# Two gated input stages of a float32 transformer kernel: their last four tiles by halves of the tokens

## The reference

```
for i in range(2):
    hn = rms_norm(h, norm_mixer[i])
    h = h + mixer_i(hn)                                  # gla, then fox
    h = h + (p[i] @ ple_proj[i]) * sigmoid(rms_norm(h, ple_norm[i]) @ ple_gate[i])
return rms_norm(h, final_norm)
```

## Time and profile before

| | |
|---|---|
| median of 3 runs | 2327.85 us (2324.41 to 2327.87) |
| profiled execution: time, span | 2328.21 us, 2326.0 us |
| mean granted TensorE clock | 0.975 of full speed |
| TensorE busy | 2200.5 us (95%) |
| VectorE busy | 1205.2 us (52%) |
| ScalarE busy | 856.5 us (37%) |
| GpSimd busy | 554.3 us (24%) |
| chain that ended last | TensorE 83%, VectorE 11%, issue 4%, ScalarE 2% |

### The profile page before, as it was taken

One profiled execution on the slowest core, in us unless ns is written; L12 is line 12 of the kernel. 1 busy time (PEld: TensorE's weight loads), 2 busy tenths in 40 slices (PEclk: granted clock), 3 DMA queues, 4 the chain that ended last, 5 costly groups with the idle time before them and its releaser, 6 DMA issues.

```text
span 2326.0 us, 29165 instructions
## 1 busy us (share of the span) xinstructions
PE 2200.5 (95%) x11168; PEld 1853.8 (80%) x11168; DVE 1205.2 (52%) x1488; ACT 856.5 (37%) x1295; POOL 554.3 (24%) x292
## 2 busy tenths in 40 slices
PE   4999999999999699999899979999999999999996
PEld 4778888988887598898778868888888888877885
DVE  6963332543331724334345454566666667676744
ACT  3136653112021323323322123446546546544311
POOL 1322221333333122222233222211111111111520
PEclk9999999999999699999999989999999999999998
DMA  8112222112331211101131121111111011012201
GB/s 338 53 46 73 73 72 73 55 37 89 137 136 46 82 36 46 37 28 46 36 138 44 46 99 56 37 46 36 45 54 43 29 54 45 27 45 101 81 19 73
DMA packets 36660, 154.59 MB, mean 66 GB/s; under 512 B 4161, under 2 KB 4161, under 8 KB 35810
## 3 DMA queue, kind: packets, MB, share of 16 engines
q1 hardware_dynamic: 23840, 93.52, 11.6%
q10 hardware_dynamic: 12738, 59.87, 7.2%
HBM read 128.15 MB, written 21.04 MB: 64 GB/s over the span
## 4 chain that ended last, share of the span: by engine, by line
PE 83%; DVE 11%; issue 4%; ACT 2%; DMA 0%; DVEq 0%; SPq 0%; ACTq 0%
PE psG L311 21%; PE psG L312 21%; PE psG L313 21%; PE psA L311 3%; PE psA L313 2%; PE psA L312 2%; PE psA L1884 1%; PE psA L1883 1%; PE psA L1858 1%; PE psA L1784 1%; DVE M L871 1%; PE psA L399 1%; DVE AL L824 1%; DVE AL L849 1%; PE psA L1867 1%
## 5 line engine op out<-in xcount | busy, mean ns | idle before, releaser
L311 PE MATMUL psG<-AH,WH 128*128 128x512 f32 x2108 | 856.8, 406 | 40.3 <-DVE AL L849 15.3
L312 PE MATMUL psG<-AL,WH 128*128 128x512 f32 x2108 | 831.8, 395 | 0.0
L313 PE MATMUL psG<-AH,WL 128*128 128x512 f32 x2108 | 830.8, 394 | 0.0
L298 POOL TENSOR_SCALAR WH<-RAW 128x1024 fp32r<-128x1024 f32 x144 | 165.3, 1148 | 1685.3 <-PE psG L311 1195.7
L311 PEld LDWEIGHTS psG<-AH,WH 128*128 128x128 f32 x2108 | 401.7, 191 | 124.7 <-issue 28.0
L313 PEld LDWEIGHTS psG<-AH,WL 128*128 128x128 f32 x2108 | 401.3, 190 | 88.1
L312 PEld LDWEIGHTS psG<-AL,WH 128*128 128x128 f32 x2108 | 402.9, 191 | 69.5
L300 POOL TENSOR_TENSOR WL<-RAW,WH 128x1024 fp32r<-128x1024 f32 x144 | 389.2, 2703 | 12.0
L2183 DVE TENSOR_TENSOR FTL<-PF,FTH 128x512 fp32r<-128x512 f32 x192 | 112.8, 588 | 129.2 <-ACT FTH L2058 127.2
L2051 ACT ACTIVATE PF<-psA,PB 128x512 f32<-128x512 f32 x192 | 111.3, 580 | 91.6 <-PE psA L1886 52.1
L2193 DVE RECIPROCAL FDR<-psA 64x128 f32<-64x128 f32 x128 | 118.2, 939 | 32.1 <-PE psA L313 30.5
(11 more groups left out here) (331 smaller groups left out, 2961.3 us busy)
## 6 DMA issues: line engine op xcount, KB each, us to landing
RAW<-w_tiles SPq DMA_DIRECT2D x144, 512.0 KB, 3.5
gates<-SIG ACTq DMA_DIRECT2D x16, 512.0 KB, 2.9
park<-X ACTq DMA_DIRECT2D x2, 4096.0 KB, 11.1
CB<-fox_c ACTq DMA_DIRECT2D x16, 512.0 KB, 4.3
X<-xT SPq DMA_DIRECT2D x4, 1024.0 KB, 11.9
WADA_SCALE<-w_ada SPq DMA_DIRECT2D x1, 4096.0 KB, 24.0
WADA_SHIFT<-w_ada SPq DMA_DIRECT2D x1, 4096.0 KB, 34.0
WADA_GATE<-w_ada ACTq DMA_DIRECT2D x1, 4096.0 KB, 16.4
```

Source lines behind the costliest of these rows:

```text
L298: nc.gpsimd.tensor_scalar(WH[:, i, :], RAW[:, i % RAW_SLOTS, :], 1.0, 0.0, ALU.mult, ALU.add).then_inc(w_high, 1)
L311: first = nc.tensor.matmul(out, wh, xh, start=start, stop=False)
L312: nc.tensor.matmul(out, wh, xl, start=False, stop=False)
L313: return first, nc.tensor.matmul(out, wl, xh, start=False, stop=stop)
```

## The change

In each of the two gated stages the first four tiles stay as they were. The last four are taken by halves of the tokens: tokens 0 to 511 of tiles 4 to 7, then tokens 512 to 1023 of tiles 4 to 7 (`step`). Each half tile is 24 + 6 matmuls, and a unit's two banks serve as two buffers of one half tile each. All four weight slots hold these tiles until their second halves; `tile_begun` is counted at the first tile's early half and at the late halves of the others.

The early half's norm is made while TensorE goes through the late half: its sums (4 blocks) stand after chunk 5 of the late half of tile 4, its spread (4 transposes) after chunk 1 of the late half of tile 5. DVE and ACT then make, between the late half's gates, the early half of the next operand (layer 0: `TN`, `AH`, `AL`) or of the final rows (layer 1), called `first(n)`.

After layer 0 the forget tile and the first q tile are also taken by halves, q two chunks behind. The late half's sums stand after chunk 3 of the early half, its spread after chunk 6; the late halves of the chunks are filled after that. After layer 1 sums, root and spread of the late half follow the last matmul, then the 8 late half rows; SP stores 16 half chunks, the early ones first. Some semaphores are merged or dropped (one name for the waits that only order POOL's and DVE's queues, `x_early` for `x_loaded`).

```diff
+    LO, HI = slice(0, HALF), slice(HALF, S)
+    WHOLE = KC // 2
+    def pe_half_sums(src, h, at):
+        for n in range(NB // 2):
+            s = (NB // 2 * h + n) * P
+            l = nc.tensor.matmul(psA[:, 2, at + n:at + n + 1], src[:, s:s + P], mat("ones")[:, 0:1], start=True, stop=True)
+        return l
+    def pe_half_spread(h):
+        for n in range(NB // 2):
+            m = NB // 2 * h + n
+            l = nc.tensor.transpose(psA[:, h, n * P:(n + 1) * P], RC[:, m:m + 1].to_broadcast([P, P]), mat("ident"))
+        return l
...
+    def pe_ple_halves(pe, layer, t0, u0):
+        gate, prod = 2 * (u0 % 2), 2 * ((u0 + 1) % 2)
+        def free(i, x):
+            if i < 2:
+                pe.wait_ge(psum_free, u0 + 2 * WHOLE - 1 + x)
+            elif i < 6:
+                pe.wait_ge(ph_free, 8 * layer + 2 * (i - 2) + 1 + x)
+            else:
+                pe.wait_ge(psum_free, u0 + 2 * (i - 2) + 1 + x)
+        for i in range(KC):
+            j, cols, b = step(i)
+            full = ph_full if i < 4 else psum_full
+            if i < 4:
+                pe.wait_ge(w_split, t0 + j + 1)
+            free(i, 0)
+            for c in range(KC):
+                f, l = half_cut(psG[:, gate + b, :], (t0 + j) % 4, c, cols)
+                if c == 0 and (i == 0 or i > 4):
+                    f.then_inc(tile_begun, 1)
+                if (i, c) == (4, 5):
+                    pe.wait_ge(lo_added, ADD_FROM + 4 * layer + 4)
+                    pe_half_sums(RS, 0, 0).then_inc(lo_sums, 1)
+                elif (i, c) == (5, 1):
+                    pe.wait_ge(lo_rec, ONE_FROM + layer + 1)
+                    pe_half_spread(0).then_inc(lo_spread, 1)
+            l.then_inc(full, 1)
+            free(i, 1)
+            js = slice(j * P, (j + 1) * P)
+            for c in range(2):
+                _, l = three(psG[:, prod + b, :], PWH[:, c, js], PWL[:, c, js], PH[:, c, cols], PL[:, c, cols], c == 0, c == 1)
+            l.then_inc(full, 1)
+    def pe_hi_sums(pe, k):
+        pe.wait_ge(sq_used, sq_base(k + 1))
+        pe_half_sums(RS, 1, 8).then_inc(sum_full, 1)
+    def pe_hi_spread(pe, k):
+        pe.wait_ge(rc_ready, k + 1)
+        pe_half_spread(1).then_inc(rs_full, 1)
...
     def pe_ple(pe, layer, t0, u0, f, k):
-        for j in range(KC):
+        for j in range(WHOLE):
...
+        pe_ple_halves(pe, layer, t0, u0)
...
     def act_ple(act, layer, u0, k, e):
-        for j in range(KC):
+        for j in range(WHOLE):
...
+        for i in range(4):
+            j, cols, b = step(i)
+            act.wait_ge(ph_free, 8 * layer + 2 * i + 1)
+            nc.scalar.activation(SG[:, b, LO], SG[:, b, LO], ACT.Sigmoid).then_inc(lo_sg, 1)
+            act.wait_ge(lo_upd, upd_from(layer) + i + 1)
+            if i < 2:
+                act.wait_ge(sq_used, sq_base(k) + j - 2)
+            else:
+                act.wait_ge(lo_added, ADD_FROM + 4 * layer + i - 1)
+            nc.scalar.activation(SQ[:, b, LO], X[:, j, LO], ACT.Square).then_inc(lo_squares, 1)
+        act.wait_ge(lo_sums, SUM_FROM + layer + 1)
+        act_half_root(0, psA[:, 2, 0:4]).then_inc(lo_root, 1)
...
+        def gate_hi(j):
+            act.wait_ge(psum_free, u0 + 2 * j + 1)
+            nc.scalar.activation(SG[:, j % 2, HI], SG[:, j % 2, HI], ACT.Sigmoid).then_inc(sg_ready, 1)
...
+        def square_hi(j):
+            act.wait_ge(x_upd, KC * e + j + 1)
+            act.wait_ge(sq_used, sq_base(k) + j - 2)
+            nc.scalar.activation(SQ[:, j % 2, HI], X[:, j, HI], ACT.Square).then_inc(sq_ready, 1)
...
+        gate_hi(4)
+        square_hi(4)
+        fill(0)
+        fill(1)
+        gate_hi(5)
...
+        fill(6)
+        fill(7)
+        gate_hi(7)
+        square_hi(7)
+        if layer == 0:
+            act_fox_in(act)
+        act.wait_ge(sum_full, k + 1)
+        act_half_root(1, psA[:, 2, 8:12]).then_inc(rms_ready, 1)
+        if layer == 0:
+            for n in range(KC):
+                act.wait_ge(tn_ready, KC * 2 + n + 1)
+                nc.scalar.activation(AH[:, n, HI], TN[:, n % 2, HI], ACT.Copy).then_inc(a_high, 1)
...
+        def add_hi(j):
+            dve.wait_ge(sq_ready, KC * k + j + 1)
+            dve.wait_ge(sq_used, sq_base(k) + j - 1)
+            nc.vector.tensor_tensor(RS[:, HI], RS[:, HI], SQ[:, j % 2, HI], ALU.add).then_inc(sq_used, 1)
...
+        def gate_hi(j):
+            dve.wait_ge(psum_full, u0 + 2 * j + 1)
+            dve.wait_ge(x_upd, KC * e + j - 1)
+            nc.vector.tensor_tensor(SG[:, j % 2, HI], psG[:, gate + j % 2, :], RSB[:, HI], ALU.mult).then_inc(psum_free, 1)
+        def prod_hi(j):
+            dve.wait_ge(sg_ready, KC * layer + j + 1)
+            dve.wait_ge(psum_full, u0 + 2 * j + 2)
+            nc.vector.tensor_tensor(SG[:, j % 2, HI], psG[:, prod + j % 2, :], SG[:, j % 2, HI], ALU.mult).then_inc(psum_free, 1)
+            dve.wait_ge(psum_free, u0 + 2 * j + 2)
+            nc.vector.tensor_tensor(X[:, j, HI], X[:, j, HI], SG[:, j % 2, HI], ALU.add).then_inc(x_upd, 1)
...
+        def first(n):
+            if layer:
+                if n < KC:
+                    nc.vector.scalar_tensor_tensor(X[:, n, LO], X[:, n, LO], col("final", n), lo, ALU.mult, ALU.mult).then_inc(x_final, 1)
+                return
+            if n < KC:
+                if n >= 2:
+                    dve.wait_ge(lo_ready, FILL_FROM + n - 1)
+                nc.vector.scalar_tensor_tensor(TN[:, n % 2, LO], X[:, n, LO], col("norm1", n), lo, ALU.mult, ALU.mult).then_inc(lo_tn, 1)
+            if n:
+                dve.wait_ge(lo_tn, FILL_FROM + n)
+                low(n - 1, LO, lo_high, lo_ready, FILL_FROM)
...
-        for j in range(KC):
+        for j in range(WHOLE):
...
-        dve_square(dve, k, KC - 1)
+        for i in range(4):
+            gate_lo(i)
+            prod_lo(i)
+            if i:
+                add_lo(i - 1)
+            else:
+                dve_square(dve, k, WHOLE - 1)
+        add_lo(3)
+        gate_hi(4)
+        dve.wait_ge(lo_root, ONE_FROM + layer + 1)
+        nc.vector.reciprocal(RC[:, 0:4], RC[:, 0:4]).then_inc(lo_rec, 1)
+        prod_hi(4)
+        dve.wait_ge(lo_spread, ONE_FROM + layer + 1)
+        first(0)
+        first(1)
+        add_hi(4)
+        gate_hi(5)
+        first(2)
+        prod_hi(5)
+        first(3)
+        first(4)
+        add_hi(5)
+        gate_hi(6)
+        first(5)
+        prod_hi(6)
+        first(6)
+        first(7)
+        first(8)
+        add_hi(6)
+        gate_hi(7)
+        prod_hi(7)
+        add_hi(7)
+        dve.wait_ge(rms_ready, k + 1)
+        nc.vector.reciprocal(RC[:, 4:8], RC[:, 4:8]).then_inc(rc_ready, 1)
+        dve.wait_ge(rs_full, k + 1)
+        if layer:
+            for n in range(KC):
+                nc.vector.scalar_tensor_tensor(X[:, n, HI], X[:, n, HI], col("final", n), hi, ALU.mult, ALU.mult).then_inc(x_final, 1)
+            return
+        for n in range(KC):
+            if n >= 2:
+                dve.wait_ge(a_ready, KC * 6 + n - 1)
+            nc.vector.scalar_tensor_tensor(TN[:, n % 2, HI], X[:, n, HI], col("norm1", n), hi, ALU.mult, ALU.mult).then_inc(tn_ready, 1)
+            if n:
+                dve.wait_ge(tn_ready, KC * 2 + n)
+                low(n - 1, HI, a_high, a_ready, KC * 6)
+        dve.wait_ge(tn_ready, KC * 2 + KC)
+        low(KC - 1, HI, a_high, a_ready, KC * 6)
...
     def pe_fox_in(pe):
-        side_by_side((T_F, U_F, T_F % 4, U_F % 2), fox_tile(0, 0), 6)
+        lag, f_at, q_at = 2, 2 * (U_F % 2), 2 * (U_FOX % 2)
+        for h, cols in enumerate((LO, HI)):
+            for n in range(KC + lag):
+                if n < KC:
+                    if h == 0 and n == 0:
+                        pe.wait_ge(w_split, T_F + 1)
+                    if n == 0:
+                        pe.wait_ge(psum_free, U_PLE0 + 13 + 2 * h)
+                    pe.wait_ge(*((a_ready, KC * 6 + n + 1) if h else (lo_ready, FILL_FROM + n + 1)))
+                    f, l = half_cut(psG[:, f_at + h, :], T_F % 4, n, cols)
+                    if h == 0 and n == 0:
+                        f.then_inc(tile_begun, 1)
+                    if h and n == KC - 1:
+                        l.then_inc(psum_full, 1)
+                if n >= lag:
+                    if h == 0 and n == lag:
+                        pe.wait_ge(w_split, T_FOX + 1)
+                    if n == lag:
+                        pe.wait_ge(psum_free, U_PLE0 + 14 + 2 * h)
+                    f, l = half_cut(psG[:, q_at + h, :], T_FOX % 4, n - lag, cols)
+                    if h and n == KC:
+                        f.then_inc(tile_begun, 1)
+                    if h and n == KC + lag - 1:
+                        l.then_inc(psum_full, 1)
+                if h == 0 and n == 3:
+                    pe_hi_sums(pe, 4)
+                elif h == 0 and n == 6:
+                    pe_hi_spread(pe, 4)
...
-    def dve_final(dve, k):
-        dve_rs(dve, k)
-        dve.wait_ge(rs_full, k + 1)
-        for j in range(KC):
```

(22 more changed lines are left out.)

## The result

The change takes 2311.09 us (median of 4 runs, 2309.1 to 2311.76) against 2327.86 for the kernel before (4 runs). The ratio is 0.9925, with a 95% interval from 0.9912 to 0.9937: faster by 16.8 us, where 20.5 were forecast, and inside the range. The profiled execution took 2311.76 us with a span of 2310.0, 16.0 less than the span of before.

A forecast was written before the change was run, and what follows sets the result against it. TensorE is busy inside gated stages, so the gain lies behind their last tiles: 12.5 us at the first stage's transition plus 8.0 at the end, 20.5 off 2327.85, giving 2307.4 us; range 2299.5 to 2315.

The forecast's parts named there:

- the shape: TensorE: no idle over 0.5 us up to the late halves, then one wait of 3 to 7 us before late sums.
- Z: Start of the first half tile, the zero of time: 1315.3 us in the first stage, 2246.8 in the second.
- B: First stage's late half: POOL does not reach DVE, or the order misses it; stall 0, 2302.4 us; chance 0.24.
- D: First stage's transition: clock stays at 1.2 GHz from the stall through the K tile's end; 2333.5 us; chance 0.02.
- E: Both stages: early norm comes with the late one, only half rows shorten the ends; near 2325 us; chance 0.03.
- the wait: First stage, before the late sums: TensorE stalls 5.0 us because POOL's splits hold DVE.
- the walk: First stage's late half: DVE's order with durations; three POOL splits hold it 1.7, 1.8 and 3.0 us, 5.7 net.
- Forget and q tile end at: After the first stage: sum placing these tiles' end at Z + 85.1, 1400.4 against 1412.9; gain 12.5 us.
- Rival C: First stage: clock falls in the stall, 2309.8 us; with all of POOL's time held, 2314.5; chance 0.21.
- What is late next: Around the K tile's start: forget chain has 3.7 us spare, X's park lands in time; nothing lost.
- the tail: End of the kernel, from the last matmul to the end: 15.4 instead of 24.8 us.

The follow-up runs named there:

- e1: Against the change: POOL's splits of the forget, q, K and V tiles write only 32 columns instead of 1024 (products not the reference's); 2303.28 us, ratio 0.9888.
- e2: Against the change: 20 matmuls into a PSUM bank that nobody reads fill TensorE's wait before the late sums; 2306.97 us, ratio 0.9908.
- e7: Only the first gated stage and the input stage behind it by halves, the second stage as in the kernel before; 2318.97 us, ratio 0.9957.
- e8: The change with e4's order, and the late half's q tile 4 chunks behind the forget tile instead of 2; 2308.37 us, ratio 0.9915.
- e5: The change with e4's DVE order and e3's late V split together; 2302.11 us, ratio 0.9887.
- e3: Against the change: POOL splits the V tile only after the last late sum on DVE; 2305.16 us, ratio 0.9903.
- e4: Against the change: the last three fills of the next norm moved later in DVE's order, two also on ACT; 2306.66 us, ratio 0.9909.

## Why the prediction was right, and where it was not

**Right: the shape.** No idle time of TensorE before Z + 59.9; sums and spreads in line (0.95 and 0.60 us forecast as 0.95 and 0.45); no wait at the early sums; no held add behind the last matmul of the second stage. Rivals B, D and E are out: the wait is there, the clock is back at full speed 7.8 us after the restart, and the early half is early.

**Right: the wait.** 5.0 us forecast, 5.01 measured, its place and its releaser (RS) too. The parts of the walk came out as well: the three splits held DVE 1.7, 1.8 and 3.0 us by the walk, and 1.7, 1.6 and 2.8 in the trace (what its held instructions take beyond 0.69). Tile 7's gate is read 5.7 us later than in e1, the walk's net figure. That the wait itself agrees to 0.01 us is luck: the gate came 0.3 us later than forecast and the last sum 0.2. e1 shows that the cause is the one named, the adds of two SBUF tensors held beside POOL's splits. The rows of before had shown it on whole tiles only; the half adds are held in the same way.

**Wrong: the clock.** The step that failed is the sum of the forecast, "Forget and q tile end at Z + 27.2 + 27.2 + 21.8 + 2.8 + 5.0 + 1.1 = Z + 85.1", which has no term for it. They end at Z + 89.2. Of the 4.1 us missing, the rows give 0.9 at the sums (1.87 against 0.95) and 2.8 in the matmuls: 6.06 us from 1382.97 to 1389.03 for 14 of them, which take 14 x 0.227 + 0.1 = 3.3 warm. e2 confirms the size by taking it away: 3.6. Rival C had the mechanism, but at 2.45 us it was too cheap: it took 3 us of half clock from the kernel before, counted from its first matmul at 1385.04, while here 5.8 us of matmuls ran at that level. Counted from the first sum pass at 1374.96, the clock of the kernel before came back only after 13 us, so its 3 us were no measure of a restart. e7 shows the spread of this term: the same code and the same wait, and 1.4 us less. With the measured 4.1 in C's place the forecast would have been 2311.5, where the median is 2311.1; the other misses, below, nearly cancel. The chance of 0.21 for it looks too low, for a row that I had read spoke for it: the kernel before, too, came out of 5.11 idle microseconds with its sums at 3.57 us instead of 1.70.

The Trainium skill, "TensorE: Matmul & The Clock Gate", Part 1, says that activity is what releases the clock. e2 agrees with that: idle time filled with junk matmuls left the granted clock at 1.00, where it was 0.68 with the hole.

**Wrong: "What is late next ... Nothing".** I followed the forget chain to its end and found 3.7 us spare there, which holds: L2095 waits for nothing. But the same sentence said that the forget tile is now full only 2.0 us before the K tile starts, and the K tile needs the PSUM unit that the forget tile fills. Two instructions must read it first, shown here on DVE and then on ACT:

```profile
1403.62 1.27 DVE L2432 TENSOR_SCALAR LF<-psG,COLS 16x1024 f32<-16x1024 f32 x1 [1.65 <-PE psG L323]
```

```profile
1404.98 1.10 ACT L2308 ACTIVATE EXF<-psG,COLS 16x1024 f32<-16x1024 f32 x1 [3.81 <-DVE LF L2432]
```

That is 2.5 us from full to free, so the last matmul of q would have been followed at 1405.39 and the next starts at 1406.23: 0.84 us. Every kernel with the new first stage has this wait but e8. Before, the unit was full at 1406.3 and the K tile began at 1412.9. The rows for this were in the prediction; I read the first as the head of a chain and not as the hold on a buffer.

**Wrong in size: the tail.** Predicted 15.4 us from the last matmul, measured 13.9. The late sums ran at 1.05 us, not 1.79, and from the end of the last row to the end of the span are 2.65 us, not 3.5. I had taken the clock as down for the sums because the kernel before had it so after 5.1 us of waiting. Here the wait is 3.0 us, and the clock fell only when the sums were through:

```profile
2300.00:2301.00 1.00, 0.43 (x4) 0.35 (x4) 0.18 (x1) 0.26 (x1) 0.00 (x0) 0.65 0.00 0
```

The window ahead of it has 1.00. The spread at 2300.84 then took 1.12 us, where a spread between warm matmuls took 0.60.

In sum: 20.5 - 4.1 (clock) - 0.84 (PSUM unit) + 1.5 (tail) - 0.9 (upstream) = 16.2 us. The spans differ by 16.0 us, the medians by 16.8.

## What to carry to other kernels

Where the trace shows one engine's instructions held by another's, price each instruction by what the other runs at that moment, and walk the order; then look whether the other engine's work is due at all: the best version here (e5) lets one split wait until the chain is through and moves three fills out of the chain's way; either alone left a wait of 2.2 us. Count a wait of TensorE together with the matmuls behind it, which may run at half speed for longer than the wait lasted. And where a tile comes closer to its reader, ask twice: when is its result needed, and who needs its buffer.

## What the runs showed of the hardware that I had not expected

The granted clock did not follow the length of the idle time in any simple way. With an idle 2.2 us it was down for 3.4 us in e3, 3.5 in e4 and 6.7 in e8; with an idle 5.0 us for 10.1 in the change and 6.8 in e7, where the code is the same. Nor did it fall at the end of the idle time: in e3, e4 and e8 it fell 0.5 to 0.7 us after TensorE had started again, at the end of the kernel 1.1 us after, and in the change 2.5 us before. So an idle 3.0 us before the last sums left those at 1.05 us, nearly the warm time, and the spread behind them had the half clock. What decides the length stays open; for a forecast I put the uncertainty at some 2 us on each such hole, an estimate from the 1.4 us between the change and e7 and the 1.6 between e4 and e8 (half of the 3.2 us more at the half clock).

What a held instruction of DVE loses follows how much of POOL's instruction is left: a 128x512 add of 0.69 us waited out the rest of a split of 2.7 us and took 2.17 to 2.87, while L1790, which reads PSUM, took 0.68 beside L310 (at 1367.30). POOL is held too, for less: L310 took 2.70 to 2.73 us when an instruction of DVE with two SBUF inputs was still running at its start, and 2.38 at 1405.73, where DVE was idle. In e4 the holding moved to the next add of the chain with its price hardly changed, 2.17 us.
